# Where the gate projection runs in a two-block decoder kernel, and how eight PSUM banks are shared

## The chip, the cores and the metric

The kernel runs on one core of a Trainium2 chip. The metric is the device time of one launch in microseconds. Engines are named as the profile names them: PE is TensorE, DVE VectorE, ACT ScalarE, POOL GpSimd, SP the engine that issues the transfers. Each runs its own instruction stream in the order in which the program wrote it, and they meet at semaphores. PE writes only to PSUM, which has eight banks of 128 x 512 fp32.

## What is computed

Two decoder blocks on one sequence of 512 tokens, width 1024. The first block (its mixer is what the change touches):

```python
h = rms_norm(x, norm_mix)
q, kc, vc, ks, vs, kw, vw, gate_logits, hq, hf, hi, hg = split(h @ w_in)
o_nsa  = nsa_mixer(...)     # per query tile of 128: compressed, selected and window branch, softmax each
# HGRN mixer, 4 heads of 128:
q = silu(hq); f = lb + (1 - lb) * sigmoid(hf); k = 1 - f; v = hi
o_hgrn = rms_norm(gated_linear_recurrence(q, k, v, log f), o_gain) * silu(hg)
x = x + concat(o_nsa, o_hgrn) @ w_out
h = rms_norm(x, norm_ffn); gate, up = split(h @ w_gate_up)
x = x + (silu(gate) * up) @ w_down
```

Then a second block of two layers: stick-breaking and differential attention, and a squared-ReLU network. All large products are fp32-accurate: each operand is split into a rounded high part and a rest, and three products are summed.

## The kernel before

**Weights.** Every weight matrix is cut into units of 128 x 1024. A unit is loaded by SP into one of four `raw` buffers, cast by ACT into `whi`, and DVE writes the rest `raw - whi` into `wlo`; there are four pairs. Units come in the order in which the products use them.

**Products.** An input projection (list `IN1`, line 353) is a group of 512 columns: `hi`, `hf`, `hq`, `hg`, `cg` (compressed keys and values, and branch gates), `q`, `kv`. A group has four tiles (`cg` three), a tile four chunks of six matmuls. A tile accumulates in bank 0 or 1 in turn. "tok" groups have tokens on the partitions, "feat" groups features.

**Order.** The order of the instructions on every engine is computed in the program: `plan_first` (line 535) lists each step with its engine, a guessed duration, what it waits for, a priority and the rings from which it takes a buffer, and `Plan.run` schedules the steps greedily, the earliest possible start first, then the priority. The starts `T[...]` then only fix the order; each engine's program (`pe_program`, `act_program` and so on) merges its parts by them. So PE takes its steps in a fixed order, and waits if one is not ready.

**First mixer.** After the norm, the groups are projected. HGRN works head by head through `STEPS`: for each head a chain of small steps on DVE (`qm`, `hT`), POOL (`km`) and ACT (`qe`, `ke`), each with one set of PE products `hp`, then the sum over the values `pv1`, its squares `hsq`, the inverse root on POOL, and `hn` on DVE (line 2088), which writes the normed head into `mixR1`. The next head's PSUM reads come after `hn` on DVE. The gate hg is evacuated by ACT as a copy into `mixR1` and a sigmoid into `sqt`, and POOL multiplies the two, then multiplies by `hgain` (function `hg` of the POOL program, line 2438). `hn` waits for all four of those tiles and multiplies them in.

q and kv pass a preparation (norm per head, split, transposes). The sparse attention (NSA) starts when `hn` of head 3 and the kv tiles are there: logits on PE (`nlg`), maximum on DVE (`nmx`), exp on ACT (`nex`), scaling on POOL (`psc`), transposes on PE (`ptr`), split by ACT and DVE (`pth`, `ptl`), and the sums (`npv`) over value tiles. A query tile and key group (qi, g) owns one sum bank until `fc` (ACT) and `fin` (DVE) have read it; there are eight of them, (0, 0) to (3, 1).

The output projection has part 0 (HGRN half of the mixer, 8 chunks of 12 matmuls) and part 1 (NSA half, 8 chunks). It uses the place of the normed input, so its tiles (`mtr`, `mTh`, `mTl`, `mSh`, `mSl`) wait for the last input chunk, `LAST_IN`. Part 0 needs only HGRN. Then come the norm `f0` and the up projection of the first block.

**Banks in the first mixer.** 0 and 1: projection tiles. 4, 5: ring `T` for transposes. 2, 3, 6: ring `L` for HGRN products and attention logits. 7 and 1: ring `O` for sums; so output chunks before the tenth use bank 0 alone, and the tenth (n == 9) waits for `fin` (3, 1). The sums take bank 1 when the projections are over.

**Places.** `sqt` is one 128 x 512 scratch buffer shared in the order of the list `SQ`; hg is among its users.

Of the kernel before, what the change touches and what calls it, by code (L numbers as in the profile page):

```python
# [11 lines left out]
ALU = mybir.AluOpType  # L12
# [191 lines left out]
def decoder_program(nc, x_d, norm_mix, w_in, q_norm, k_norm, cmp_pos_k, cmp_pos_v, cmp_k_w1, cmp_k_w2,  # L204
# [86 lines left out]
    p1 = [r.t("p1_%d" % i, [128, 512]) for i in range(3)]  # L291
    r = Region(at_h, at_w)
    t1 = [(r.t("t1h%d" % i, [128, 512], F32R), r.t("t1l%d" % i, [128, 512], F32R)) for i in range(4)]
    p1 += [r.t("p1_%d" % i, [128, 512]) for i in range(3, 6)]
# [53 lines left out]
    def rows(w, nk):  # L348
        for k in range(nk):
# [29 lines left out]
    def dA(n):  # L379
        return 0.07 + 0.00084 * n  # L380
# [58 lines left out]
    SQ = [("hq", h) for h in range(4)] + [("hg", t) for t in range(4)] + [("q", t) for t in range(4)] + [("kv", t) for t in range(4)] + \  # L439
# [53 lines left out]
    def plan_op(P, m, fin, ring0):  # L493
        mk = "m%d" % m
        for n, (t, half, part) in enumerate([(t, half, 0) for half in range(2) for t in range(4)] + [(t, half, 1) for t in range(4) for half in range(2)]):
            unit = U["op", m, part, half]
            P.add(("op", (m, t, half, part)), "PE", 2.72, ("wlo", unit), ("wlo", unit + 1), *[("mSl" if part else "mTl", (mk, t, j)) for j in ((0, 1) if part else (2, 3))],
                  ("fin", (3, 1)) if m == 0 and n == 9 else None, seq="op", take=[(ring0 if n < 8 else "G", [("xadd", ("op", m, t, half, part))])])
# [13 lines left out]
    def plan_up(P, m):  # L512
        for part in range(2):
            for j in range(4):
                for i in range(4):
                    unit = U["up", m, 0] + j
                    P.add(("up", m, 0, part, i, j), "PE", 0.72, ("wlo", unit), *[("hTl", ("f%d" % m, t, 1)) for t in (2 * part, 2 * part + 1)], seq="gemm_up")
                    U_mm[unit] = ("up", m, 0, part, i, j)
# [14 lines left out]
    LAST_IN = {m: ("in", (m, "S1" if m else "kv", 3, 3)) for m in range(3)}  # L533

    def plan_first():
        P = Plan(T)
        P.ring("T", 2)
        P.ring("L", 3)
        P.ring("O", 2)
        P.rings["G"] = (2, [[("evV", (0, "hi", 0))], [("evV", (0, "hi", 1))]])  # L540
        P.ring("B0", 1)
# [10 lines left out]
        def sq_free(user):  # L552
            n = SQ.index(user)
            return (None if n == 0 else ("evV", (0,) + SQ[n - 1]) if SQ[n - 1][0] == "hq" else ("hgg", SQ[n - 1][1]) if SQ[n - 1][0] == "hg" else
                    ("fin", SQ[n - 1][1:]) if SQ[n - 1][0] == "fin" else ("psr", SQ[n - 1]))

        def evacs(name, i):
            k = (0, name, i)
            return [("evA", k)] if name in ("hf", "hg", "q") or (name, i) == ("cg", 2) else [("evV", k)] if name in ("hi", "hq") else [("evA", k), ("evV", k)]
        plan_in(P, 0, "n1", evacs)  # L560

        for i in range(4):
# [6 lines left out]
            P.add(("evA", (0, "hg", i)), "ACT", 2 * dA(512), last[3], sq_free(("hg", i)), pri=2)  # L569
            P.add(("hgg", i), "POOL", 2.6, ("evA", (0, "hg", i)))  # L570
# [47 lines left out]
        for h, lv in STEPS:  # L618
            k, before = (h, lv), (h, lv - 1)
            if lv < 0:  # L620
                P.add(("hk", h), "DVE", 0.46, ("fd", h), *([("hp", (h - 1, 5)), ("km", (h - 1, 6)), ("ke", (h - 1, 6))] if h else []), seq="hgrn", pri=4)
                P.add(("hp", k), "PE", 0.95, ("hk", h), ("evV", (0, "hq", h)), seq="hgrnT", pri=3, take=[("L", [("att", k)])])
                P.add(("att", k), "DVE", dV(512), ("hp", k), ("pv1", h - 1) if h else None, seq="hgrnV", pri=3)
            elif lv < 9:
# [11 lines left out]
                P.add(("hp", k), "PE", 0.95, ("qm", k), *([("km", k), ("qe", k), ("ke", k)] if lv else []), seq="hgrnT", pri=3, take=[("L", [("att" if lv < 7 else "aoc", k)])])  # L636
# [4 lines left out]
            else:  # L641
                P.add(("pv1", h), "PE", 2.6, ("att", (h, 6)), ("aoc", (h, 8)), *[("evV", (0, "hi", t)) for t in range(4)], seq="hgrnT", pri=3, take=[("L", [("hn", h)])])
# [7 lines left out]
        for it in NSA:  # L650
            i, qi, g, N, nh = it["i"], it["qi"], it["g"], it["N"], it["nh"]
            np_ = len(it["parts"])
            if it["kind"] == "cmp":
                if g == 0:
                    last = max([o["i"] for o in NSA if o["kind"] == "cmp" and o["qi"] == qi - 1], default=None)
                    P.add(("nlg", (i, 0)), "PE", 2.0, ("kch", 0), ("vcl", 0), ("pcpA", ("q", qi)), ("pcpV", ("q", qi)), *first, seq="nlg", pri=3, take=[("L", [("cad", qi)])])
# [5 lines left out]
            else:  # L662
                n = 0
                for r_, hs in enumerate(it["banks"]):
                    k = (i, r_)
                    P.add(("nlg", k), "PE", 0.09 + len(hs) * 2 * (N / 2400 + 0.014), ("pcpA", ("q", qi)), ("pcpV", ("q", qi)), ("pcpA", ("kv", qi)), ("pcpV", ("kv", qi)), *first,
                          seq="nlg", pri=3, take=[("L", [("nex", k)])])
# [17 lines left out]
        plan_op(P, 0, lambda kind, j, t: ("hn", 2 * j + 1) if kind == "D" else ("fin", (t, j)), "B0")  # L685
# [1935 lines left out]
```

## Time and profile before

| | us |
|---|---|
| median of 3 runs | 1974.48 (1973.38 to 1975.92) |
| the profiled execution | 1971.68 |
| its span | 1970.0 |
| PE matmul busy | 1933.9 (98%) |
| PE weight loads busy | 1622.3 (82%) |
| DVE busy | 968.8 (49%) |
| ACT busy | 790.6 (40%) |
| POOL busy | 257.5 (13%) |

The rows are of one execution. Busy time of PE is that of matmuls whose ends are modelled: a matmul of 512 columns shows 0.39 us and the next one starts 0.227 us after it, so small gaps do not show as idle, and start-to-start distances tell more. "[idle before <-releaser]" behind a row is time in which the engine stood still, and what ended it. Rows "x6" are merged. The granted clock is in shares of full speed, so 0.50 is 1.2 GHz and 1.00 is 2.4 GHz. Stages of the first mixer by the span's time: projections with HGRN from 12 to 222 us, attention 222 to 349, the rest of the output projection and the norm to about 380, the first block's network to 770; the second block's two layers follow.

### The profile page before, as it was taken

The page shows a single profiled execution, that of the slowest core. Times are in us where ns is not written, and L with a number is a line of the kernel's source. Part 1 is how long each engine was busy: PE and PEld are TensorE (multiplying, and loading weights), DVE is VectorE, ACT ScalarE, POOL GpSimd, SP SyncE. Part 2 cuts the span into 40 slices and gives each one's busy share as a digit, 9 for nine tenths or more (in the row PEclk, how much of TensorE's full clock was granted, in tenths as well). Part 3 has the DMA queues.
Part 4 walks back from the last instruction along what each step waited for, and adds up shares of the span by engine and source line. Part 5 has one row for each costly group of instructions (what it writes and reads, how often), then busy time and mean ns, then how long its engine had stood idle before and what let it go on. Part 6 is the DMA issues. An engine that isn't in the chain of part 4 may idle for free.

```text
span 1970.0 us, 24643 instructions
## 1 busy us (share of the span) xinstructions
PE 1933.9 (98%) x9842; PEld 1622.3 (82%) x9842; DVE 968.8 (49%) x1555; ACT 790.6 (40%) x1406; POOL 257.5 (13%) x334
## 2 busy tenths in 40 slices
PE   9999999999999999999999999999999899999998
PEld 7888787888888888877888888888878788888887
DVE  5546688432223357588642233337668852223334
ACT  4435566322223234377432332223547633333222
POOL 2133245000000010001011220001001102221000
PEclk9999999999999999999999999999999999999999
DMA  7211300133333322221133333332121123333331
GB/s 235 67 54 55 112 22 33 55 117 97 97 99 93 97 78 75 84 86 43 54 107 97 96 96 97 97 96 82 59 86 44 48 93 115 98 97 94 98 97 54
DMA packets 97138, 167.79 MB, mean 85 GB/s; under 512 B 8160, under 2 KB 49152, under 8 KB 97024
## 3 DMA queue, kind: packets, MB, share of 16 engines
q1 hardware_dynamic: 97024, 166.21, 27.5%
q8 instruction: 78, 1.28, 0.3%
q14 instruction: 36, 0.29, 0.0%
HBM read 164.09 MB, written 2.10 MB: 84 GB/s over the span
## 4 chain that ended last, share of the span: by engine, by line
PE 90%; DVE 5%; ACT 3%; issue 1%; DMA 0%; POOL 0%; SPq 0%; DVEq 0%; POOLq 0%; ACTq 0%
PE ps L49 86%; PE ps L52 4%; DVE wlo L71 1%; ACT sk1h L65 1%; DVE p L91 1%; DVE hTl L71 1%; ACT whi L65 0%; ACT p L62 0%; DVE x L71 0%; DVE t1l L71 0%; DVE small L82 0%; DMA raw<-in_w_in_dram 0%; DVE rot L71 0%; ACT hTh L65 0%; ACT t1h L65 0%
## 5 line engine op out<-in xcount | busy, mean ns | idle before, releaser
L65 ACT ACTIVATE whi<-raw 128x1024 fp32r<-128x1024 f32 x294 | 309.8, 1055 | 745.4 <-PE ps L49 742.5
L71 DVE TENSOR_TENSOR wlo<-raw,whi 128x1024 fp32r<-128x1024 f32 x294 | 361.3, 1230 | 417.2 <-ACT whi L65 414.5
L49 PE MATMUL ps<-hTh,whi 128*128 128x512 f32 (+1 forms) x1176 | 442.8, 377 | 0.0
L49 PE MATMUL ps<-hTh,wlo 128*128 128x512 f32 (+1 forms) x1176 | 438.0, 372 | 0.0
L49 PE MATMUL ps<-hTl,whi 128*128 128x512 f32 (+1 forms) x1176 | 437.9, 372 | 0.0
L49 PE MATMUL ps<-whi,uh 128*128 128x512 f32 x688 | 268.1, 390 | 0.0
L49 PE MATMUL ps<-whi,ul 128*128 128x512 f32 x688 | 267.8, 389 | 0.0
L49 PE MATMUL ps<-wlo,uh 128*128 128x512 f32 x688 | 267.8, 389 | 0.0
L49 PEld LDWEIGHTS ps<-hTh,wlo 128*128 128x128 f32 x1176 | 220.8, 188 | 39.6
L49 PEld LDWEIGHTS ps<-hTl,whi 128*128 128x128 f32 x1176 | 221.1, 188 | 36.9
L49 PEld LDWEIGHTS ps<-hTh,whi 128*128 128x128 f32 x1176 | 221.0, 188 | 36.6
L49 PE MATMUL ps<-whi,hTh 128*128 128x512 f32 x576 | 235.3, 409 | 3.0 <-DVE mixLT L71 1.6
L49 PE MATMUL ps<-whi,hTl 128*128 128x512 f32 x576 | 226.4, 393 | 0.0
L49 PE MATMUL ps<-wlo,hTh 128*128 128x512 f32 x576 | 225.8, 392 | 0.0
L71 DVE TENSOR_TENSOR ul<-u,uh 128x512 fp32r<-128x512 f32 x86 | 60.9, 711 | 281.2 <-ACT uh L65 281.2
L49 PEld LDWEIGHTS ps<-whi,uh 128*128 128x128 f32 x688 | 129.2, 188 | 26.8
L49 PEld LDWEIGHTS ps<-wlo,uh 128*128 128x128 f32 x688 | 129.2, 188 | 26.7
L49 PEld LDWEIGHTS ps<-whi,ul 128*128 128x128 f32 x688 | 129.2, 188 | 26.6
L49 PEld LDWEIGHTS ps<-whi,hTh 128*128 128x128 f32 x576 | 109.2, 190 | 24.3 <-DVE hTl L71 2.0
L49 PEld LDWEIGHTS ps<-whi,hTl 128*128 128x128 f32 x576 | 108.7, 189 | 23.9
L49 PEld LDWEIGHTS ps<-wlo,hTh 128*128 128x128 f32 x576 | 109.4, 190 | 19.2
L71 POOL TENSOR_TENSOR u<-gtmp 128x512 f32<-128x512 f32 x64 | 81.3, 1274 | 265.7 <-ACT gtmp L62 265.7
(232 smaller groups left out, 2156.7 us busy)
## 6 DMA issues: line engine op xcount, KB each, us to landing
raw<-in_w_ff_dram SPq DMA_DIRECT2D x128, 512.0 KB, 3.7
raw<-in_w_gate_up_dram SPq DMA_DIRECT2D x88, 256.0 KB, 3.1
raw<-in_w_in_dram SPq DMA_DIRECT2D x40, 512.0 KB, 4.5
raw<-in_w_in_dram SPq DMA_DIRECT2D x68, 256.0 KB, 3.1
raw<-in_w_down_dram SPq DMA_DIRECT2D x22, 512.0 KB, 3.6
raw<-in_w_o_dram SPq DMA_DIRECT2D x16, 512.0 KB, 3.7
x<-in_x_dram SPq DMA_DIRECT2D x8, 512.0 KB, 6.9
raw<-in_w_out_dram SPq DMA_DIRECT2D x8, 512.0 KB, 5.0
```

Of the source, the lines that this page charges most:

```text
L49: return self.eng.matmul(out, l, r, start=start, stop=stop, skip_group_check=True)
L52: return self.eng.transpose(out, in_, idn)
L65: return self.eng.activation(out, in_, ACT.Copy)
L71: return self.eng.tensor_tensor(out, a, b, op)
L91: return self.eng.tensor_tensor_scan(out, a, zero, 1.0, ALU.mult, ALU.add)
```

## The change

The group hg becomes the last of the input projections. Its sigmoid goes into one of two new buffers `sg`, DVE multiplies it by the tile in PSUM into the same buffer, and POOL multiplies `mixR1` by it once `hn` of head 3 is done. `hn` multiplies by `hgain` itself and no longer waits for the gate. The rings `T` and `L` become one ring of five banks in rotation; the sums have bank 7 alone; the output projection has banks 0 and 1 from its first chunk, and the wait for `fin` (3, 1) stands before the up projection and the transposes of norm `f0`. The load of the norm's gain is issued after `plo` (kv, 3) and not after the first chunk of part 1.

```diff
-    IN1 = [("hi", "tok", 4, [(2328, 512)]), ("hf", "feat", 4, [(1816, 512)]), ("hq", "feat", 4, [(1304, 512)]),
-           ("hg", "tok", 4, [(2840, 512)]), ("cg", "feat", 3, [(512, 256), (1280, 24)]), ("q", "tok", 4, [(0, 512)]),
-           ("kv", "tok", 4, [(768, 512)])]
+    IN1 = [("hi", "tok", 4, [(2328, 512)]),
+           ("hf", "feat", 4, [(1816, 512)]),
+           ("hq", "feat", 4, [(1304, 512)]),
+           ("cg", "feat", 3, [(512, 256), (1280, 24)]),
+           ("q", "tok", 4, [(0, 512)]),
+           ("kv", "tok", 4, [(768, 512)]),
+           ("hg", "tok", 4, [(2840, 512)])]
...
-    LAST_IN = {m: ("in", (m, "S1" if m else "kv", 3, 3)) for m in range(3)}
+    LAST_IN = {m: ("in", (m, "S1" if m else "hg", 3, 3)) for m in range(3)}
...
-        P.ring("T", 2)
-        P.ring("L", 3)
-        P.ring("O", 2)
+        P.ring("T", 5)
+        P.ring("O", 1)
         P.rings["G"] = (2, [[("evV", (0, "hi", 0))], [("evV", (0, "hi", 1))]])
-        P.ring("B0", 1)
...
-            P.add(("evA", (0, "hg", i)), "ACT", 2 * dA(512), last[3], sq_free(("hg", i)), pri=2)
-            P.add(("hgg", i), "POOL", 2.6, ("evA", (0, "hg", i)))
+            P.add(("evA", (0, "hg", i)), "ACT", dA(512), last[3], ("cm", (1, 3)), ("hgg", i - 2) if i >= 2 else None, pri=2)
+            P.add(("evV", (0, "hg", i)), "DVE", dV(512), ("evA", (0, "hg", i)), pri=2)
+            P.add(("hgg", i), "POOL", 1.0, ("evV", (0, "hg", i)), ("hn", 3), pri=4)
...
-                P.add(("hn", h), "DVE", 1.1, ("rs", ("hc", h)), *[("hgg", t) for t in range(4)], seq="hgrnV", pri=3)
+                P.add(("hn", h), "DVE", 1.1, ("rs", ("hc", h)), seq="hgrnV", pri=3)
...
-                yield T["op", (m, 0, 0, 1)] + 0.1
-                sp.wait_ge(*at("mm", ("op", m, 0, 0, 1)))
+                yield T["op", (m, 0, 0, 1)] + 0.1 if m else T["plo", ("kv", 3)] + 1.0
+                sp.wait_ge(*(at("mm", ("op", m, 0, 0, 1)) if m else at("plo", ("kv", 3))))
...
-        tring, lring, oring = Ring([4, 5]), Ring([2, 3, 6]), Ring([7, 1])
+        tring, lring, oring = Ring([4, 5, 2, 3, 6]), Ring([2, 3]), Ring([7])
+        fring = Ring([4, 5])
...
-                b = n % 2 if m or part else 0
+                b = n % 2
...
-                if m == 0 and n == 9:
-                    pe.wait_ge(*at("fin", (3, 1)))
...
+                            if j == 0 and g == 0 and m == 0:
+                                pe.wait_ge(*at("fin", (3, 1)))
...
-                        pe.wait_ge(*at("hn", 2 * j - 3))
+                        pe.wait_ge(*at("hgg", t))
...
-                    act.copyA(mixR1[:, i, :], ps[b][:, :]).then_inc(*up("hgc", i))
-                    sq_free(("hg", i))
-                    act.act(sqt[:, :], ps[b][:, :], ACT.Sigmoid).then_inc(*up("evA", key))
+                    if i >= 2:
+                        act.wait_ge(*at("hgg", i - 2))
+                    else:
+                        act.wait_ge(*at("cm", 1))
+                    act.act(sg[i % 2][:, :], ps[b][:, :], ACT.Sigmoid).then_inc(*up("evA", key))
...
+                elif name == "hg":
+                    dve.wait_ge(*at("evA", key))
+                    dve.tt(sg[i % 2][:, :], ps[b][:, :], sg[i % 2][:, :], ALU.mult).then_inc(*up("evV", key))
...
-                    for t in range(4):
-                        dve.wait_ge(*at("hgg", t))
+                    dve.wait_ge(*at("c", "all"))
                     c = cell(0, ("hc", h), 4)
                     for t in range(4):
-                        mr = mixR1[:, t, 128 * h:128 * h + 128]
-                        ins = dve.stt(mr, ps[bank("h", h, 9)][:, 128 * t:128 * t + 128], c[:, t:t + 1], mr, ALU.mult, ALU.mult)
+                        ins = dve.stt(mixR1[:, t, 128 * h:128 * h + 128], ps[bank("h", h, 9)][:, 128 * t:128 * t + 128], c[:, t:t + 1], hgain[:, :],
+                                      ALU.mult, ALU.mult)
...
-                pool.wait_ge(*at("evA", (0, "hg", t)))
-                pool.wait_ge(*at("hgc", t))
-                pool.tt(mixR1[:, t, :], mixR1[:, t, :], sqt[:, :], ALU.mult).then_inc(*up("hgm", t))
-                pool.wait_ge(*at("hgm", t))
-                pool.wait_ge(*at("c", "all"))
-                m3 = mixR1[:, t, :].rearrange("p (h d) -> p h d", h=4)
-                pool.tt(m3, m3, bc(hgain[:, :], 1, [128, 4, 128]), ALU.mult).then_inc(*up("hgg", t))
+                pool.wait_ge(*at("evV", (0, "hg", t)))
+                pool.wait_ge(*at("hn", 3))
+                pool.tt(mixR1[:, t, :], mixR1[:, t, :], sg[t % 2][:, :], ALU.mult).then_inc(*up("hgg", t))
```

## Rows read from the trace of the kernel before

**Rows 1.** The page: shares of the chain that ended last.

```profile
PE 90%; DVE 5%; ACT 3%; issue 1%; DMA 0%; POOL 0%; SPq 0%; DVEq 0%; POOLq 0%; ACTq 0%
```

**Rows 2.** Windows: stretch, length, busy of each engine, PE clock, DMA share, GB/s.

```profile
60.00:222.00 162.00, 161.72 (x948) 137.52 (x947) 93.24 (x198) 74.30 (x179) 50.41 (x63) 1.00 0.23 74
222.00:349.00 127.00, 117.83 (x742) 97.77 (x740) 97.06 (x220) 82.15 (x220) 51.46 (x57) 0.96 0.11 38
...
281.90:305.00 23.10, 23.10 (x134) 20.01 (x133) 16.73 (x30) 11.19 (x24) 7.28 (x8) 1.00 0.15 45
250.00:280.00 30.00, 28.33 (x193) 23.57 (x194) 27.91 (x72) 24.27 (x71) 15.70 (x18) 1.00 0.00 1
...
232.50:238.40 5.90, 5.90 (x22) 5.05 (x21) 1.89 (x9) 4.16 (x22) 3.13 (x3) 0.50 0.00 0
```

**Rows 3.** Timeline of PE, one cycle of query tile 3: start, length, instruction.

```profile
330.36 0.48 PE L49 MATMUL ps<-khh,qst 128*128 128x512 f32 x1
330.67 0.40 PE L49 MATMUL ps<-kll,qst 128*128 128x512 f32 x1
330.90 0.28 PE L49 MATMUL ps<-t1h,vst 128*128 128x256 f32 x1
...
331.38 0.60 PE L52 MATMUL ps<-ident,p 128*128 128x128 f32 x4
331.82 0.22 PE L49 MATMUL ps<-m_causal,identB 128*128 128x128 bf16 x1
```

**Rows 4.** Timeline of PE: HGRN; compressed keys' transposes; an output chunk, 302.30 to 305.02.

```profile
94.91 1.00 PE L49 MATMUL ps<-hQ,hK 128*128 128x64 f32 x8
...
121.97 1.11 PE L49 MATMUL ps<-hQ,hK 128*128 128x64 f32 x8
...
202.89 0.33 PE L52 MATMUL ps<-identR,kst 64*128 64x64 f32 x2
...
302.30 0.39 PE L49 MATMUL ps<-whi,hTh 128*128 128x512 f32 x1
...
305.02 0.28 PE L49 MATMUL ps<-t1h,vst 128*128 128x256 f32 x1
```

**Rows 5.** Groups by form, PE, 222.3 to 349.2: count | busy, mean ns | idle.

```profile
L52 PE MATMUL ps<-ident,p 128*128 128x128 f32 x160 | 25.8, 280 | 0.5 <-DVE hTl L71 0.5
L49 PE MATMUL ps<-t1h,vst 128*128 128x256 f32 x72 | 21.0, 312 | 2.3 <-DVE t1l L71 1.8
...
L49 PE MATMUL ps<-whi,hTh 128*128 128x512 f32 x36 | 15.3, 425 | 0.0
```

**Rows 6.** Timeline of PE: the longest wait; the last sums and what follows.

```profile
231.94 0.61 PE L49 MATMUL ps<-m_causal,identB 128*128 128x512 bf16 x1 [1.81 <-ACT p L62]
...
347.39 0.28 PE L49 MATMUL ps<-t1l,vst 128*128 128x256 f32 x1
349.23 0.50 PE L49 MATMUL ps<-whi,hTh 128*128 128x512 f32 x1 [1.56 <-DVE mixLT L71]
```

**Rows 7.** Timeline of DVE: `hn` of head 0.

```profile
120.79 1.13 DVE L79 SCALAR_TENSOR_TENSOR mixR<-ps,small,mixR 128x128 f32<-128x128 f32 x4 [1.29 <-POOL mixR L71]
```

**Rows 8.** Groups by form, 92 to 122: gate product, weight rest, hq.

```profile
L71 POOL TENSOR_TENSOR mixR<-mixR,sqt 128x512 f32<-128x512 f32 x4 | 5.2, 1293 | 11.7 <-ACT sqt L62 11.7
...
L71 DVE TENSOR_TENSOR wlo<-raw,whi 128x1024 fp32r<-128x1024 f32 x1 | 1.2, 1226 | 0.3 <-ACT whi L65 0.3
...
L71 DVE TENSOR_TENSOR hq<-ps,sqt 128x512 f32<-128x512 f32 x1 | 0.7, 692 | 1.9 <-ACT sqt L62 1.9
```

**Rows 9.** Timeline of POOL: an hgain product; a `wlo` ran from 118.12 to 119.50.

```profile
118.98 1.67 POOL L71 TENSOR_TENSOR mixR<-mixR,hgain 128x512 f32<-128x512 f32 x1
```

**Rows 10.** Timeline of ACT: the table load before the first exp.

```profile
39.07 1.28 ACT L62 ACT_TABLE_LOAD   x1
...
227.13 1.28 ACT L62 ACT_TABLE_LOAD   x1
228.43 0.42 ACT L62 ACTIVATE p<-p 128x256 f32<-128x256 f32 x1
```

More of the change, by code:

```diff
@@ L491, in plan_in, with plan_op @@
             U_mm[unit] = ("in", m, name, i, j)
-    def plan_op(P, m, fin, ring0):
+    def plan_op(P, m, fin):
         mk = "m%d" % m
@@ L497, in plan_op @@
             P.add(("op", (m, t, half, part)), "PE", 2.72, ("wlo", unit), ("wlo", unit + 1), *[("mSl" if part else "mTl", (mk, t, j)) for j in ((0, 1) if part else (2, 3))],
-                  ("fin", (3, 1)) if m == 0 and n == 9 else None, seq="op", take=[(ring0 if n < 8 else "G", [("xadd", ("op", m, t, half, part))])])
+                  seq="op", take=[("G", [("xadd", ("op", m, t, half, part))])])
             P.add(("xadd", ("op", m, t, half, part)), "DVE", dV(512), ("op", (m, t, half, part)), ("x", ("r", t)) if m == 0 and part == 0 else None,
@@ L516, in plan_up @@
                     unit = U["up", m, 0] + j
-                    P.add(("up", m, 0, part, i, j), "PE", 0.72, ("wlo", unit), *[("hTl", ("f%d" % m, t, 1)) for t in (2 * part, 2 * part + 1)], seq="gemm_up")
+                    P.add(("up", m, 0, part, i, j), "PE", 0.72, ("wlo", unit), *[("hTl", ("f%d" % m, t, 1)) for t in (2 * part, 2 * part + 1)],
+                          ("fin", (3, 1)) if m == 0 else None, seq="gemm_up")
                     U_mm[unit] = ("up", m, 0, part, i, j)
@@ L641, in plan_first @@
             else:
-                P.add(("pv1", h), "PE", 2.6, ("att", (h, 6)), ("aoc", (h, 8)), *[("evV", (0, "hi", t)) for t in range(4)], seq="hgrnT", pri=3, take=[("L", [("hn", h)])])
+                P.add(("pv1", h), "PE", 2.6, ("att", (h, 6)), ("aoc", (h, 8)), *[("evV", (0, "hi", t)) for t in range(4)], seq="hgrnT", pri=3, take=[("T", [("hn", h)])])
                 P.add(("hsq", h), "ACT", 1.3, ("pv1", h), seq="hgrnA", pri=3)
                 P.add(("rs", ("hc", h)), "POOL", 1.2, ("hsq", h), pri=1)
-                P.add(("hn", h), "DVE", 1.1, ("rs", ("hc", h)), *[("hgg", t) for t in range(4)], seq="hgrnV", pri=3)
+                P.add(("hn", h), "DVE", 1.1, ("rs", ("hc", h)), seq="hgrnV", pri=3)
         for t in range(4):
@@ L655, in plan_first @@
                     last = max([o["i"] for o in NSA if o["kind"] == "cmp" and o["qi"] == qi - 1], default=None)
-                    P.add(("nlg", (i, 0)), "PE", 2.0, ("kch", 0), ("vcl", 0), ("pcpA", ("q", qi)), ("pcpV", ("q", qi)), *first, seq="nlg", pri=3, take=[("L", [("cad", qi)])])
+                    P.add(("nlg", (i, 0)), "PE", 2.0, ("kch", 0), ("vcl", 0), ("pcpA", ("q", qi)), ("pcpV", ("q", qi)), *first, seq="nlg", pri=3, take=[("T", [("cad", qi)])])
                     P.add(("cad", qi), "DVE", 0.9, ("nlg", (i, 0)), ("ptr", (last, 0)) if qi else None, seq="nmx", pri=3)
@@ L854, in ev @@
         key = (m, name, i)
-        if name in ("hf", "hg", "q") or (name, i) == ("cg", 2) or (name in ("vD", "vS") and i % 2):
+        if name in ("hf", "q") or (name, i) == ("cg", 2) or (name in ("vD", "vS") and i % 2):
             return [("evA", key)]
@@ L1095, in norm @@
                     else:
-                        b, before = tring.take(("hTl", (key, t, half)))
+                        ring = fring if key == "f0" else tring
+                        if t == half == 0:
+                            fring.reset(("fin", (3, 1)), ("mTl", ("m0", 3, 3)))
+                        b, before = ring.take(("hTl", (key, t, half)))
                         for done in before:
@@ L1207, in hgrn @@
                 rel = ("hn", h) if lv == 9 else ("aoc", (h, lv)) if lv >= 7 else ("att", (h, lv))
-                b, before = lring.take(rel)
+                b, before = tring.take(rel)
                 for done in before:
@@ L1262, in nsa_logits @@
                     yield T["nlg", (it["i"], 0)]
-                    b, before = lring.take(("cad", qi))
+                    b, before = tring.take(("cad", qi))
                     for done in before:
@@ L1280, in nsa_logits @@
                     yield T["nlg", (i, r_)]
-                    b, before = lring.take(("nex", (i, r_)))
+                    b, before = tring.take(("nex", (i, r_)))
                     for done in before:
@@ L1910, in evac1 @@
             for name, kind, i, n, used in chunks(0):
-                if name in ("hf", "hg", "q") or (name, i) == ("cg", 2):
+                if name in ("hf", "q") or (name, i) == ("cg", 2):
                     continue
```

43 lines of the change are left out of this document (18 added, 25 removed).

## The prediction

> **What bounds the kernel now.** I read the page's busy table and chain first. TensorE's matmuls are busy for 98% of the span, as the table says, and it holds 90% of the chain that ended last [rows 1]. So time can come only from stretches in which TensorE does less than it could. The windows by stage show where they are: from 222 to 349 us, the sparse attention (NSA), matmuls are busy for 117.8 of 127 us and the granted clock is 0.96, while 281.9 to 305, where output-projection chunks lie between the attention steps, has no idle at all [rows 2]. After 372 us nothing that the change touches runs; its 1,600 us I take as equal.
>
> Busy time hides small gaps, because ends are modelled. So I counted the work of 222.3 to 349.2 by start-to-start distances. A full cycle of the last query tile [rows 3] gives 0.31 us for a khh matmul of 512 columns, 0.23 for the kll one, 0.12 for each 256-column sum, 0.44 for four transposes. A projection matmul takes 0.227: an output chunk of twelve runs from 302.30 to 305.02 [rows 4]. Times the counts, whose three largest forms are [rows 5]: 160 transposes 17.6 us, 144 sum matmuls 17.3, 109 projection matmuls (nine chunks of the output projection, 2.72 us each) 24.7, the 16 + 16 logit matmuls of 512 columns 8.6, 64 of the compressed keys at 0.11 7.1, 16 + 16 of 384 columns 7.0 (0.26 + 0.18), and the 18 smaller forms, some 200 instructions, 23.6. Sum 106 of 126.9 us: **21 us in which TensorE works below what its instructions need**. Named waits explain part (1.81 and 1.56 us, [rows 6]), half-rate clock another: the 5.9 us from 232.5 to 238.4 ran at a granted 0.50, that is 1.2 GHz, a loss of 3.0 [rows 2]. It came behind the wait that ended at 231.94.
>
> A second wait costs nothing today but sets the order. The four-head HGRN chain issues its matmuls at 94.91, then none until 121.97 [rows 4], because DVE's `hn` of head 0 (line 2088) waits for the POOL gate product of the last token tile [rows 7]: 16 gate chunks had to come first. TensorE is full meanwhile (161.7 of 162 us from 60 to 222, [rows 2]), so that stall is worth zero by itself.
>
> **The change part by part.** *Gate projection last.* 16 chunks of 6 matmuls, half an output chunk each, 16 x 1.36 = 21.8 us, leave the full stretch before the attention and enter the one with gaps. Since `hn` no longer needs the gate, head 1 goes on 27 us earlier (121.97 - 94.91, [rows 4]) and all heads are done well before kv, so q and kv end at 222.3 - 21.8 = 200.5 and the attention starts there. TensorE's total work is the same; what changes is how much of the 21 us is filled.
>
> *Is there enough filler?* Attention work without output chunks is 106 - 24.7 = 81 us. Filler is now gate 21.8, output part 0 21.8, and part 1 of token tiles 0 to 2 16.3: before, bank 1 belonged to the sums and the ninth output chunk was the last that could run before `fin` (3, 1); the change moves that wait to the up projection. Sum 141 us from 200.5, to 341.5, then 5.4 us of tile 3, against 349.2 plus seven chunks (19.0) before: 346.9 against 368.2, which is the 21 us again. The attention chain by itself took 127 us, less than 141, so TensorE sets the end, if its order written by the planner finds each step ready.
>
> *What cannot be filled.* The slice with filler had 0 idle, the dense 250 to 280 us 1.7 in 30 [rows 2]. I take the middle, 0.28 us per 10, over 141 us: 3.9, and the last handover to the mixer tiles, 1.8 [rows 6]. Together 5.7; bounds 1.8 and 9.8.
>
> *Other engines.* DVE takes four products from PSUM (0.69 each like hq's) and four wlo (1.23 each): 7.7 us more beside its 97.1 of 127 [rows 2, 8], now over 141: 74%, dense but with room. `hn` only changes an operand. ACT loses four copies and gains four weight casts in the stretch, and was busy for 82 of 127 us [rows 2]. POOL drops the four hgain products and does the other four (1.29 each, [rows 8]) after `hn`, hidden: its 51.5 us of the stretch leave it idle for over half. Behind a POOL wait for `hn` (3) or the gate stand the attention's scalings, but `hn` (3) is early then. SP: the reload of x waits for `pv1` (3) and comes earlier, the gain load moves to `plo` (kv, 3); the weights queued behind these waits have theirs met by then. Each zero; a late unit would cost its landing time.
>
> While POOL ran the hgain products, one that met a DVE wlo took 1.67 us, where the gate products take 1.29 [rows 8, 9]; that is 0.4 a meeting, at most 1.6 us in four, off the path. The Trainium skill, SBUF — State Buffer, section Who interferes with whom, says that a DVE tensor_tensor with both inputs in SBUF and a reading GpSimd instruction fully block each other; the four moved products would by that hold DVE for up to 5.2 us. The row shows a part of that.
>
> *The table loads, the cost that the diff does not show.* The gate's sigmoid now runs between the attention's exps. The trace has one ACT table load at 227.13, 1.28 us, just before the first exp, and none between 39 and 227 although sigmoid, square, tanh and copy alternate there [rows 10]. Each gate tile between exps costs two loads, four tiles 8 more: 8 x 1.28 = 10.3 us on ACT. TensorE's order is fixed and planned without them, so a late exp shows up as a wait there, like the 1.81 us at 231.94, the first logits behind that load. A step ready early waits up to one chunk of 1.36 us for TensorE, which hides some. Bounds: 0 and 10.3 exposed; I take half, 5.1. And one chance in two of a half-rate dip of 3.0 us: 1.5 (bounds 0 and 6, two dips).
>
> *Banks.* Five shared in rotation instead of 3 + 2: the same number, zero, bounds -1 and +2. One bank for sums: each of seven handovers needs ACT's copy and DVE's product, 347.39 to 349.23 in the trace [rows 6], 1.84 us; with filler to issue I take zero, the upper bound is a rival.
>
> Sum: 21 - 5.7 - 5.1 - 1.5 = 8.7 us. Span 1970.0 - 8.7 = 1961.3; the profiled execution took 1971.7 and the median of the runs is 1974.5, so I subtract from the median: 1965.8, and give **1966.0 us**.
>
> **The rivals.** (A) The loads hide under gate chunks and the clock stays up: 21 - 5.7 = 15.3, 1959.2; if even the filling is perfect, 1955.5. For it: ACT has 45 idle us in 127. Against: the 1.81 us wait behind the only load.
> (B) Every load is exposed and two dips follow, a wait on ACT's exps in the place of the gaps that the chunks fill: 21 - 5.7 - 10.3 - 6.0 = -1.0, 1975.5, reaching down to 1970. For it: fixed order, and the row at 231.94. Against: exps that wait behind TensorE anyway. The Trainium skill, ScalarE: Activation LUTs, section What ACT_TABLE_LOAD costs, gives 2.66 us for a switch with its drain. By it the eight cost 21.3 us, and all exposed the kernel would come out at about 1987. In this trace 1.30 us pass from the load's start to the exp's [rows 10], so the row speaks for half of that.
> (C) It does not do what it says: the attention starts no earlier, because PE's order takes gate chunks ahead of the compressed keys' transposes (202.89 us now, [rows 4]), and the gate simply precedes it: gain about 0, 1974.5.
> (D) Slower: the single sum bank. If each of seven handovers stalls TensorE for 1.84 us, 12.9 us go and 1966.0 becomes 1978.9; with a half-rate loss of 3.0 behind each, 34 us and 2000. It decides from 1.8 us each (8.7 + 3.9 = 12.6 us over seven). For it: from 250 to 280 DVE is 93% busy [rows 2], so its part of the handover can queue. Against: filler exists now at each.
>
> **How the numbers follow.** Forecast 0.50 (1960 to 1970), A 0.15, B 0.17, C 0.05, D 0.13. A measurement of this kernel tells 0.2%, 3.9 us, from no change. Faster than 1970.5: 0.50 + 0.15 + 0.02 of B = 0.67; within: 0.15 of B + 0.05 = 0.20; slower: 0.13. Range 1956 to 1976: it leaves out D and the tips of A and B, 0.17.
>
> **What would show it.** HGRN matmuls without a gap after 95 us and done before 170; first logits near 201 to 203; gate chunks between logits from 201 on; output chunks up to about 340; up to nine table loads from 200 to 245, and TensorE waits on ACT's exps near them. Part 1 of the output projection running before the last sums shows the freed bank. Wrong would be: logits starting after 210, TensorE waits for mixLT at each handover, a granted clock of 0.5 over more than 6 us, or any change after 372 us other than the shift.

## The result, and the profile after

The changed kernel takes 1961.24 us (median of four executions, 1960.28 to 1964.64); the kernel before, beside it, takes 1974.97 (1973.38 to 1975.92). The ratio is 0.9934 [0.9917, 0.9952], 13.0 us less. The prediction said 1966.0 with 1956 to 1976. Its profiled execution took 1961.46, of which the span is 1959.7, 10.3 less than the span before.

Busy times and chain of the page, kernel after (against [rows 1]):

```profile
PE 1930.2 (98%) x9842; PEld 1620.1 (83%) x9842; DVE 972.0 (50%) x1559; ACT 798.7 (41%) x1410; POOL 252.1 (13%) x330
...
PE 90%; DVE 4%; ACT 4%; issue 1%; DMA 0%; POOL 0%; SPq 0%; DVEq 0%; POOLq 0%; ACTq 0%
```

As before, these two lines say nothing of where the 10 us went. The windows by stage do (start:end and length, then busy time and count of PE, PEld, DVE, ACT and POOL, the granted clock, the DMA share and GB/s), kernel after:

```profile
60.00:200.00 140.00, 139.56 (x851) 119.28 (x850) 86.97 (x194) 65.87 (x166) 40.16 (x55) 1.00 0.23 71
200.00:280.00 80.00, 75.74 (x492) 62.78 (x491) 62.84 (x140) 63.94 (x160) 33.07 (x35) 1.00 0.17 53
280.00:345.00 65.00, 64.79 (x377) 55.17 (x376) 45.37 (x90) 35.50 (x81) 24.27 (x28) 0.97 0.14 41
```

The full stretch now ends near 200 instead of 222. What follows is the attention with its chunks: 4.5 us of idle in the 145 from 200 to 345, nearly all of it ahead of 280, where [rows 2] has 9.2 in 127; the clock is 1.00 and 0.97, against 0.96.

Timeline of PE, kernel after (start, length, instruction, idle before it and its releaser): the end of HGRN, the last transposes of kv, the first logits, the last two groups of sums, and the last transposes but one of norm `f0`:

```profile
164.14 0.83 PE L49 MATMUL ps<-hv,AO 128*128 128x128 f32 x6
...
201.55 0.50 PE L52 MATMUL ps<-identR,sth 128*128 128x128 f32 x4 [0.64 <-DVE stl L71]
...
203.69 0.48 PE L49 MATMUL ps<-kch,qst 128*128 128x32 f32 x3
...
341.20 0.28 PE L49 MATMUL ps<-t1l,vst 128*128 128x256 f32 x1
...
344.06 0.28 PE L49 MATMUL ps<-t1h,vst 128*128 128x256 f32 x1
...
344.54 0.40 PE L49 MATMUL ps<-whi,hTh 128*128 128x512 f32 x1
...
368.94 0.63 PE L52 MATMUL ps<-ident,htmp 128*128 128x128 f32 x4 [0.63 <-DVE htmp L79]
```

HGRN's last matmuls end at 165.0. The first logits of kch come at 203.69, where they came at 223.68 before: 20 us earlier. The sums end at 344.5 with eleven of sixteen output chunks issued (before: nine, at 347.5). The wait of 1.56 us behind the last sums in [rows 6] is gone: between 341.32 and 344.06 lies an output chunk, and at 344.54 the next one begins at once. The transposes of norm `f0` that stand at 368.94 stood at 379.23 before, 10.3 us later, and from there to the end both kernels take the same 1,590.8 us, as the prediction assumed.

### The profile page after: what moved, and what is told of

The parts are those of the page before. It is cut to its first block, busy times and chain, and to the rows that moved or that the text cites. A ratio compares the mean times of both kernels' runs of the same rounds, so it can differ in the third digit from the quotient of the medians.

```text
span 1959.7 us, 24657 instructions
## 1 busy us (share of the span) xinstructions
PE 1930.2 (98%) x9842; PEld 1620.1 (83%) x9842; DVE 972.0 (50%) x1559; ACT 798.7 (41%) x1410; POOL 252.1 (13%) x330
## 3 DMA queue, kind: packets, MB, share of 16 engines
q8 instruction: 78, 1.28, 0.3%
## 4 chain that ended last, share of the span: by engine, by line
PE 90%; DVE 4%; ACT 4%; issue 1%; DMA 0%; POOL 0%; SPq 0%; DVEq 0%; POOLq 0%; ACTq 0%
PE ps L49 86%; PE ps L52 4%; DVE wlo L71 1%; ACT p L62 1%; ACT sk1h L65 1%; ACT whi L65 1%; DVE p L91 1%; ACT L62 0%; DVE hTl L71 0%; DMA raw<-in_w_in_dram 0%; DVE x L71 0%; DVE rot L71 0%; ACT t1h L65 0%; ACT htmB L62 0%; ACT hTh L65 0%
## 5 line engine op out<-in xcount | busy, mean ns | idle before, releaser
L65 ACT ACTIVATE whi<-raw 128x1024 fp32r<-128x1024 f32 (+1 forms) x294 | 309.7, 1055 | 744.8 <-PE ps L49 741.2
L71 DVE TENSOR_TENSOR wlo<-raw,whi 128x1024 fp32r<-128x1024 f32 (+1 forms) x294 | 360.7, 1228 | 398.4 <-ACT whi L65 396.0
```

Source lines behind the costliest of these rows:

```text
L65: return self.eng.activation(out, in_, ACT.Copy)
L71: return self.eng.tensor_tensor(out, a, b, op)
```

## The experiments

Each ratio below is against the kernel before on the same chip, with its interval, and the us of a gain or a loss are worked out from the ratio; the two medians beside it can differ by another number. A difference of two ratios is uncertain by 3 to 4 us. I go first after the loads, then after the order and the banks. The changed kernel was timed once more, as the partner of the other runs.

> The changed kernel once more, as the base of this group of runs: 1961 us within 2 us, a gain of 13.7 us over the kernel before, if the first result holds.

Measured: 1963.3 us against 1973.63, ratio 0.9954 [0.9939, 0.9968], 9.1 us less; span 1959.5, the same picture. Together with the first timing the gain is between 9 and 13 us. The two intervals overlap; comparisons with the other experiments use this one.

### The table loads

**Without a table switch, sigmoid left out.** This kernel stores a copy in place of the sigmoid, so the gate isn't that of the reference; everything else stands.

```diff
-                    act.act(sg[i % 2][:, :], ps[b][:, :], ACT.Sigmoid).then_inc(*up("evA", key))
+                    act.copyA(sg[i % 2][:, :], ps[b][:, :]).then_inc(*up("evA", key))
```

> The changed kernel with a plain copy in the place of the gate's sigmoid, so the eight extra table loads are gone and nothing else in the order of the work changes. This leaves the sigmoid out of the computation. If the loads are hidden (rival A): 1961, no difference. If half of their 10.3 us is exposed, as the sum had it: 1956. If all is exposed (rival B) and the half-rate stretch behind the waits goes too: 1951 or less.

**The same product from tanh.** x · sigmoid(x) = x · (1 + tanh(x / 2)) / 2; the half goes into the HGRN norm's mean square and its eps.

```diff
-                    act.act(sg[i % 2][:, :], ps[b][:, :], ACT.Sigmoid).then_inc(*up("evA", key))
+                    act.act(sg[i % 2][:, :], ps[b][:, :], ACT.Tanh, scale=0.5).then_inc(*up("evA", key))
...
-                    dve.tt(sg[i % 2][:, :], ps[b][:, :], sg[i % 2][:, :], ALU.mult).then_inc(*up("evV", key))
+                    dve.stt(sg[i % 2][:, :], sg[i % 2][:, :], 1.0, ps[b][:, :], ALU.add, ALU.mult).then_inc(*up("evV", key))
...
-                rsqrt(cell(0, ("hc", h), 4), 1.0 / 128, ("hc", h))
+                rsqrt(cell(0, ("hc", h), 4), 4.0 / 128, ("hc", h), 4.0 * EPS)
```

> The changed kernel with the sigmoid as (1 + tanh(x/2)) / 2: ACT computes the tanh, DVE's one instruction adds 1 and multiplies by the tile in PSUM, and the factor 1/2 goes into the root of the HGRN norm on POOL. If tanh shares a table with exp, the eight loads go and the time is that of the copy version within 1 us. If it does not, the loads stay and the time is 1961.

**Eight more loads.** A sigmoid and an exp of one column ahead of each gate sigmoid.

```diff
+                    one = nsm[:, 52 + i:53 + i]
+                    act.act(one, ps[b][:, 0:1], ACT.Sigmoid).then_inc(*up("tiny"))
+                    act.wait_ge(sems.get("tiny", "tiny"), count["tiny"])
+                    act.act(one, one, ACT.Exp).then_inc(*up("tiny"))
+                    act.wait_ge(sems.get("tiny", "tiny"), count["tiny"])
                     act.act(sg[i % 2][:, :], ps[b][:, :], ACT.Sigmoid).then_inc(*up("evA", key))
```

> The changed kernel with one more pair of table loads for each gate tile (a one-column sigmoid and a one-column exp ahead of the gate's sigmoid): eight more loads, 10.3 us of ACT, and some 2 us of tiny instructions and waits. Loads hidden: within 2 us of 1961. Half exposed: 1967. Fully exposed: 1973 or more.

Measured: copy 0.9921 [0.9906, 0.9936], 1956.14 us; tanh 0.9922 [0.9906, 0.9937], 1956.4; eight more 1.0025 [1.0015, 1.0035], 1977.64. Timeline of ACT, kernel after, the loads around the first gate tile and the last:

```profile
213.60 1.28 ACT L62 ACT_TABLE_LOAD   x1
214.90 0.60 ACT L62 ACTIVATE sg<-ps 128x512 f32<-128x512 f32 x1
215.51 1.28 ACT L62 ACT_TABLE_LOAD   x1
216.81 0.37 ACT L62 ACTIVATE p<-ps,small 128x128 f32<-128x128 f32 x1
...
277.77 1.28 ACT L62 ACT_TABLE_LOAD   x1
279.07 0.58 ACT L62 ACTIVATE p<-ps,small 128x384 f32<-128x384 f32 x1
```

The groups by form of ACT from 200 to 345 us (count | busy, mean ns | idle) have this line in the kernel after:

```profile
L62 ACT ACT_TABLE_LOAD x9 | 11.5, 1283 | 0.2
```

and this one in the tanh kernel:

```profile
L62 ACT ACT_TABLE_LOAD x1 | 1.3, 1283 | 0.0
```

So the change adds exactly eight loads, two a gate tile, 10.3 us of ACT. PE's longest wait in the attention comes behind the last of them. Timeline of PE, kernel after, with the window that follows it:

```profile
277.92 0.39 PE L49 MATMUL ps<-t1h,vst 128*128 128x256 f32 x1 [0.72 <-DVE t1l L71]
...
279.79 0.66 PE L52 MATMUL ps<-ident,p 128*128 128x128 f32 x4 [1.37 <-ACT p L62]
...
281.76 0.69 PE L52 MATMUL ps<-ident,mixR 128*128 128x128 f32 x2 [0.19 <-ACT p L62]
```

```profile
280.00:290.00 10.00, 9.79 (x61) 8.67 (x60) 7.28 (x20) 6.21 (x20) 5.35 (x8) 0.83 0.18 52
```

The load at 277.77 holds the exp until 279.07, its transposes start at 279.79 after 1.37 us of wait, and the granted clock of the next ten microseconds is 0.83, which is a third of them at 1.2 GHz and 1.7 us lost. In the tanh kernel there is no such wait for an exp, but one of about the same length 2.6 us earlier, for `hTl` of DVE:

```profile
277.19 0.72 PE L52 MATMUL ps<-ident,mixR 128*128 128x128 f32 x4 [1.45 <-DVE hTl L71]
```

The last section says what held DVE there. The clock stays at 1.00 behind it, so a wait of this length need not bring the lower clock. The windows 200 to 280 and 280 to 345 of the tanh kernel read:

```profile
200.00:280.00 80.00, 77.53 (x522) 66.30 (x520) 66.07 (x149) 58.16 (x165) 37.25 (x40) 1.00 0.19 60
280.00:345.00 65.00, 65.00 (x373) 55.11 (x373) 44.95 (x86) 33.39 (x70) 22.19 (x27) 1.00 0.11 33
```

The eight loads are worth 0.9954 - 0.9922 = 0.0032, 6.3 us, and the means of the two kernels, timed side by side, differ by 6.4. Copy and tanh agree, so it is the loads and not the sigmoid's arithmetic. Eight further ones cost 1.0025 - 0.9954 = 0.0071, 14.0 us, more than their own 10.3. The edit adds more than loads: eight one-column instructions and the waits for them. In all ACT needs 4.29 us from the first load to the gate's sigmoid (213.47 to 217.76) where the kernel after needs 1.30, so 3.0 a tile or 12.0 in four. PE's waits of over 2 us from 200 to 345 in that kernel, and a window of it:

```profile
221.23 0.28 PE L49 MATMUL ps<-m_cmp,identB 128*128 128x256 bf16 x1 [2.91 <-ACT p L62]
...
244.78 0.58 PE L49 MATMUL ps<-t1h,vst 128*128 128x256 f32 x1 [2.81 <-DVE t1l L71]
...
276.70 0.39 PE L49 MATMUL ps<-t1h,vst 128*128 128x256 f32 x1 [3.29 <-DVE t1l L71]
...
295.01 0.39 PE L49 MATMUL ps<-t1h,vst 128*128 128x256 f32 x1 [3.79 <-DVE t1l L71]
```

```profile
240.00:260.00 20.00, 17.19 (x97) 15.51 (x96) 12.38 (x28) 14.03 (x32) 5.03 (x6) 0.74 0.00 1
```

One wait for each of the four gate tiles, 12.8 us together, and the clock falls to 0.74 behind the second; behind each of the other three follow 3 us or more at a mean of 0.54 to 0.58. From 200 to 380 us PE is idle for 3.1 us in the tanh kernel, 5.1 in the kernel after and 14.8 here. So the first eight loads partly hide in slack; the next eight find little left, and the clock's loss comes on top.

### The gate's place and the banks

**Banks alone.** The kernel before with the changed kernel's ring of five, its one sum bank and its two banks for all output chunks; the gate stays fourth.

```diff
-        P.ring("T", 2)
-        P.ring("L", 3)
-        P.ring("O", 2)
+        P.ring("T", 5)
+        P.ring("O", 1)
...
-        tring, lring, oring = Ring([4, 5]), Ring([2, 3, 6]), Ring([7, 1])
+        tring, lring, oring = Ring([4, 5, 2, 3, 6]), Ring([2, 3]), Ring([7])
+        fring = Ring([4, 5])
```

> The kernel before with the new banks alone: one ring of five, one bank for sums, output chunks on banks 0 and 1 with the wait for the last sums moved to the up projection. The gate projection stays fourth, and hn waits for it. By the filler account the five output chunks that may now run before the attention's end (13.6 us) fill the last query tile, and no table load is added: a gain of 8 to 11 us over before, 1963 to 1966. If the gate chunks are what fills the gaps (rival): 2 us or less. If the single sum bank stalls at its handovers (rival D): slower than before.

**Gate ahead of kv.** The changed kernel with its gate group one place earlier: HGRN is freed, yet all gate chunks precede the attention and no sigmoid falls between exps.

```diff
-           ("kv", "tok", 4, [(768, 512)]),
-           ("hg", "tok", 4, [(2840, 512)])]
+           ("hg", "tok", 4, [(2840, 512)]),
+           ("kv", "tok", 4, [(768, 512)])]
```

> The changed kernel with the gate projection before kv and not behind it: HGRN is freed from the gate and the banks are new, but no gate chunk lies in the attention, and its sigmoids come before the first exp, so there are no extra table loads. If HGRN's 27 us stall is worth nothing by itself, this is the time of the new banks alone within 1.5 us. If freeing HGRN helps by itself, it is faster than that by 3 us or more.

Measured: banks alone 0.9996 [0.9987, 1.0005], gate ahead of kv 0.9998 [0.9988, 1.0007]. To within 2 us neither does anything. In the second, HGRN's matmuls end at 164.9, as in the changed kernel: the removed stall of 27 us is worth zero, as predicted. The 8 to 11 us that I expected of the banks alone did not come. Both kernels have the same tail: 14 output chunks are issued before the sums end, and these end at 359.5. That is 12 us later than before, for five more output chunks of 2.72 us, 13.6 us in all: the chunks pushed the attention back nearly by their own length and did not fill its gaps. Timeline of PE, banks alone, the last sum and the waits of over 1.5 us after it:

```profile
359.44 0.28 PE L49 MATMUL ps<-t1l,vst 128*128 128x256 f32 x1
361.28 1.16 PE L52 MATMUL ps<-ident,htmp 128*128 128x128 f32 x8 [1.56 <-DVE mixLT L71]
...
372.71 0.66 PE L52 MATMUL ps<-ident,htmp 128*128 128x128 f32 x4 [1.93 <-DVE hTl L71]
```

The 32 us around the end of the attention as a window, first banks alone, then the kernel after:

```profile
344.00:376.00 32.00, 25.81 (x159) 21.23 (x158) 23.84 (x41) 20.36 (x39) 10.36 (x14) 0.95 0.17 53
```

```profile
329.00:361.00 32.00, 32.00 (x173) 27.23 (x172) 21.25 (x31) 15.15 (x25) 6.50 (x11) 1.00 0.13 35
```

With the shared ring, transposes of the mixer tiles get a bank early, so PE takes output chunks early, and by 344 only two of sixteen are left. The last tile's attention and the norm then run bare: 6.2 us of idle in 32, at a lower clock. In the kernel after, the gate chunks take the early places, five output chunks are left, and there is no idle.

**Separate rings again.** The changed kernel with transposes on banks 4 and 5 and logits on 2, 3 and 6; one sum bank.

```diff
-        tring, lring, oring = Ring([4, 5, 2, 3, 6]), Ring([2, 3]), Ring([7])
+        tring, lring, oring = Ring([4, 5]), Ring([2, 3, 6]), Ring([7])
```

> The changed kernel with the five banks split again, two for transposes and three for HGRN products and logits; one bank for sums. The sum gave the shared ring zero with bounds of -1 and +2, so 1962 to 1965. If sharing is what let the work interleave: slower than the changed kernel by 4 us or more.

**Two sum banks.** Ring of four, sums on 7 and 6:

```diff
-        tring, lring, oring = Ring([4, 5, 2, 3, 6]), Ring([2, 3]), Ring([7])
+        tring, lring, oring = Ring([4, 5, 2, 3]), Ring([2, 3]), Ring([7, 6])
```

> The changed kernel with two banks for sums (7 and 6) and a shared ring of four. If the handovers of the single sum bank cost nothing, as the sum had it, and a fifth bank in the ring matters little: 1963 within 2 us. If the handovers cost 1.8 us each (rival D): some 10 us faster than the changed kernel. If the ring needs its fifth bank: slower by 3 us or more.

**Ring of four, one sum bank.** Bank 6 is left unused:

```diff
-        tring, lring, oring = Ring([4, 5, 2, 3, 6]), Ring([2, 3]), Ring([7])
+        tring, lring, oring = Ring([4, 5, 2, 3]), Ring([2, 3]), Ring([7])
```

> The changed kernel with a ring of four banks (4, 5, 2, 3), bank 6 unused, one bank for sums. With the version that gives bank 6 to a second sum (1.0011 of before) it separates the two. If the single sum bank costs nothing: the same as that version within 2 us, and the fifth ring bank is worth some 10 us. If the second sum bank helps: slower than it by 3 us or more.

Measured: separate rings 0.9994 [0.9984, 1.0004]; two sum banks 1.0011 [1.0001, 1.0020]; ring of four 1.0010 [0.9999, 1.0020]. The last two differ only in the second sum bank, and agree within their intervals: the second sum bank is worth nothing here, and rival D is out. The fifth bank of the ring is worth 1.0010 - 0.9954 = 0.0056, 11 us, and sharing it 0.9994 - 0.9954 = 0.0040, 7.9 us. The small cost that the sum gave to the banks failed in both. The two losses look different. With the ring of four, the picture is that of banks alone: a wait of 4.03 us for ACT's p at 271.62, sums until 362.7, 14 output chunks before, then 1.57 and 2.17 us bare. With separate rings it is the other way round, as its timeline of PE and its windows before and after the last sums show:

```profile
333.83 0.38 PE L52 MATMUL ps<-ident,mixR 128*128 128x128 f32 x2
335.47 0.39 PE L49 MATMUL ps<-t1h,vst 128*128 128x256 f32 x1 [1.25 <-DVE t1l L71]
```

```profile
280.00:336.00 56.00, 51.82 (x304) 43.36 (x304) 37.52 (x84) 30.95 (x77) 23.71 (x26) 0.89 0.00 1
336.00:361.00 25.00, 25.00 (x115) 20.71 (x115) 12.29 (x17) 6.22 (x8) 1.49 (x3) 1.00 0.28 85
```

Output part 0 needs the transposes of the mixer tiles, sixteen of mixR. The tile view of PE for mixR, 200 to 345 us (count, duration, first and last start), with separate rings:

```profile
L52 PE MATMUL ps<-ident,mixR x16: 270/273/474, 281.8 to 333.9; 128*128 128x128 f32 x16
```

and in the kernel after:

```profile
L52 PE MATMUL ps<-ident,mixR x16: 272/310/473, 275.9 to 287.2; 128*128 128x128 f32 x16
```

They share banks 4 and 5 with the attention's transposes and take 52 us, from 281.8 to 333.9; in the ring of five they take 11, from 275.9 to 287.2. It is the same with the gate fourth: 52 us in the kernel before, with two banks (223.4 to 275.9), 11 with banks alone (224.5 to 236.0). Two banks did no harm as long as these transposes could start with the attention; now they wait for the last gate chunk. Only three output chunks are there for the attention, whose gaps stay open (4.2 us idle in 56, clock 0.89; this execution has a mean clock of 0.993 and took 1974.99 us, the slowest of eleven, so its clock is worse than the kernel's usual one), and thirteen run in one full block afterwards, when PE needs no filler.

**Separate rings without loads.** The tanh kernel with separate rings:

> The version without extra table loads (sigmoid through tanh) with the five banks split again into two and three. If the split rings lose because the mixer tiles' transposes cannot get a bank, the loss against the shared ring stays at some 10 us: 1966. If the split only lost because late exps held its banks, without the loads it loses under 3 us: 1957 to 1959.

Measured: 0.9957 [0.9944, 0.9971] (1965.12 us), 0.0035 or 6.9 us more than tanh on the shared ring. So the ring's worth does not hang on the loads, though 6.9 is less than the "some 10" expected.

**A planner that knows the loads.** The guessed duration of the gate's sigmoid raised by two loads:

```diff
-            P.add(("evA", (0, "hg", i)), "ACT", dA(512), last[3], ("cm", (1, 3)), ("hgg", i - 2) if i >= 2 else None, pri=2)
+            P.add(("evA", (0, "hg", i)), "ACT", dA(512) + 2.56, last[3], ("cm", (1, 3)), ("hgg", i - 2) if i >= 2 else None, pri=2)
```

> The changed kernel, with the sigmoid, and a planner that counts 2.56 us more for each of the four gate sigmoids, so that TensorE's order leaves room for the two table loads. If the loads cost because the fixed order does not know them, most of their 7 us comes back: 1957 to 1959. If ACT's time itself is what costs: 1962 to 1964, no change.

Measured: 0.9994 [0.9985, 1.0002], 0.0040 or 7.9 us worse than the changed kernel, where a gain was expected. The gate ends earlier (the first mixer transposes at 255.4 instead of 275.9), 14 output chunks go ahead of the last sums at 355.7, and the tail is bare again, with waits of 2.29, 1.03, 1.57 and 2.02 us from 348 to 369.

**Tanh with the gate chunks first.** The tanh kernel, and the plan's priority for gate chunks 4 instead of 5:

```diff
-                  seq="gemm", take=[("G", evacs(name, i))] if j == 0 and (m or used >= 4) else ())
+                  seq="gemm", pri=4 if (m, name) == (0, "hg") else 5, take=[("G", evacs(name, i))] if j == 0 and (m or used >= 4) else ())
```

> The tanh version with the gate chunks at priority 4 in the plan where other projection chunks have 5. Gate chunks then go ahead of steps of priority 5 that are ready at the same time, and the output chunks can start earlier. If the stall at 270 to 280 us, where the gate ends and the output tiles are not ready, is what is left: up to 2 us faster than 1956. If chunks too early only delay the attention: the same or slower.

Measured: 0.9914 [0.9900, 0.9927] (1956.15 us), not to be told from tanh alone. These two are the fastest versions that compute the whole, 15 to 17 us below the kernel before.

### All executions, split by the clock

Each execution comes with its time and PE's mean granted clock. (1 - clock) x time is what PE lost at most to the half rate; the rest is the time without it. Means over all executions of a kernel (the clock is known to 0.001, 2 us in one execution, which averages out). The end of the sums and the output chunks behind it are those of the profiled execution:

| kernel | n | sums end | output chunks after | time | lost to clock | rest |
|---|---|---|---|---|---|---|
| before (with the first four experiments) | 17 | 347.5 | 7 | 1972.5 | 11.8 | 1960.6 |
| before (with the middle four) | 33 | 347.5 | 7 | 1973.4 | 13.2 | 1960.3 |
| before (with the last four) | 21 | 347.5 | 7 | 1973.4 | 13.2 | 1960.2 |
| after, first timing | 4 | 344.5 | 5 | 1961.9 | 6.4 | 1955.5 |
| after, again | 6 | 344.3 | 5 | 1963.3 | 7.9 | 1955.4 |
| copy, sigmoid left out | 6 | 340.6 | 5 | 1956.9 | 5.2 | 1951.7 |
| tanh | 6 | 339.1 | 5 | 1956.9 | 5.5 | 1951.4 |
| tanh, gate chunks first | 4 | 340.8 | 5 | 1956.6 | 5.4 | 1951.2 |
| tanh, rings apart | 5 | 326.6 | 13 | 1964.9 | 5.9 | 1959.0 |
| eight more loads | 12 | 362.2 | 5 | 1977.7 | 14.5 | 1963.2 |
| banks alone | 11 | 359.5 | 2 | 1972.5 | 11.1 | 1961.3 |
| gate ahead of kv | 11 | 359.5 | 2 | 1972.8 | 10.8 | 1962.1 |
| rings apart | 11 | 336.1 | 13 | 1971.3 | 9.7 | 1961.6 |
| two sum banks | 11 | 355.9 | 2 | 1974.4 | 10.6 | 1963.8 |
| ring of four | 11 | 362.7 | 2 | 1975.5 | 10.8 | 1964.7 |
| planner knows loads | 11 | 355.7 | 2 | 1972.1 | 10.6 | 1961.5 |

The rest scatters little within a kernel (standard deviation 0.2 to 2.1 us). In the second timing a little over half of the changed kernel's gain is in it, 1960.6 - 1955.4 = 5.2 us. The other 11.8 - 7.9 = 3.9 us are clock: PE waits less and spends less time at 1.2 GHz. For the first timing no clocks of its partner are on record. The kernels with 2 or 13 chunks behind the sums all have a larger rest than the changed kernel with its 5, and those with the sigmoid also lose more to the clock; tanh with 13 has 7.6 us more rest than tanh with 5. But the number of chunks doesn't settle the rest: the kernel before has 7 and its rest is 5 us larger, and eight more loads cost 7.8 us of rest with 5.

## Why the prediction was right

**The start of the attention** moved as worked out: 20 us earlier for 21.8 predicted, first logits at 203.69 for "201 to 203". `hn` no longer waits for the gate, and that alone is worth zero.

**The filling** was the main term, 21 - 5.7 = 15.3 us. The tanh kernel shows it without the loads: 0.9922 is 15.4 us. That the two agree so closely is in part luck. By the table 9.2 us of it are rest and 6.3 clock, while the 21 held 3.0 of clock, so more was expected of the filling and less of the clock. And the agreement holds for the whole package only. The filler count of 141 us against an attention of 127 treated the gate and the output chunks as one sum, good wherever they lie. The runs show that it isn't so: banks alone added output chunks to the attention and gained 0; gate ahead of kv likewise; and with separate rings the same 141 us are on hand and 7 to 8 us of the gain are gone. The count also had 14 output chunks ahead of the last sums and 2 behind them. The changed kernel has 11 and 5, and every kernel here that does have 14 and 2 is no faster than the kernel before. What counts is when a chunk can be issued and, as far as the windows show, how many are left at the end.

**Banks** is therefore the step that failed: "five shared in rotation instead of 3 + 2: the same number, zero, bounds -1 and +2". Undoing the sharing costs 7.9 us, 6.9 without loads. I counted banks, and not who asks for them and when. The trace before had the mixer tiles' transposes spread over 52 us from the attention's first step on, and this could have been read: started behind the last gate chunk, at 276 to 282, the same 52 us end at 330, too late for part 0 to fill anything. The total came out because the 15.3 had silently assumed that output part 0 would be ready in time, which only the shared ring makes true.

**The single sum bank** at zero was right: the second one changes 1.0010 to 1.0011. PE's waits in the whole trace of after name no reader of the sums but `mixLT`, with 0.2 us against 1.6 before: none of the seven handovers stalls PE. That filler at each is the reason fits the timeline of the last one, and wasn't tested at the others.

**The table loads.** Count and length were right (eight, 1.28 us), the exposed share was taken as half, 5.1 us, with 1.5 for a dip of the clock behind them. Together 6.6; measured 6.3 by the ratios. By the table 4.0 of it are rest (1955.4 against 1951.4) and 2.4 clock, so both terms were near. That they lie between 213 and 278 instead of 200 and 245 is a miss: the gate chunks are spread over 70 us among the logits, and not issued in a row. The Trainium skill, ScalarE: Activation LUTs, section What ACT_TABLE_LOAD costs, has 1283 ns for the load, which the rows confirm, and 2.66 us for a switch with its drain, which they do not: from load to sigmoid pass 1.30 us (213.60 to 214.90) and from load to exp again 1.30 (215.51 to 216.81).

**The clock** was under-priced as a term. I weighed one dip of 3.0 us at one half and counted the 3.0 of the trace before within the 21. Over many executions the kernel before loses 12 to 13 us of its whole time to the lower clock. Its profiled execution, with a mean clock of 0.995, loses at most 9.9, of which two stretches in the attention are 5; a single trace shows one draw. This may be why the first timing gained 13.0 us and the spans of the two profiled executions differ by 10.3.

**POOL beside DVE.** The prediction read one hgain product of 1.67 us as a block in part, 0.4 a meeting, and left the other side out: the DVE subtraction beside it, of 560 columns, took 1.38 us (118.12), and one with no product beside it 0.74 (115.85). In the changed kernel one of the four moved products meets a subtraction, and it costs DVE 0.9 us (rows in the last section). That is less than the 5.2 of the upper bound, but whether it lies off the path, as predicted, was not tested.

The forecast of the sum was 8.7 us. The second timing gives 9.1 and the first 13.0; the forecast lies within the interval of the second (6.3 to 12.0 us) and just outside that of the first (9.5 to 16.4).

**Open.** The planner's greedy order turns small changes of a guessed duration or a ring into 2, 5 or 13 chunks behind the sums. That the number of chunks left is the cause, and not a companion, is argued from the windows; a kernel that fixes this number by hand with all else equal wasn't tried. Nor was the gate last tried with all banks as before: the version with separate rings keeps one sum bank and two banks for the output chunks. The kernel with two sum banks ran its profiled execution in 1968.7, 7 us below its own median, with a clock of 0.998 against 0.993 to 0.997 in the others. Its time without the clock's loss is that of the others, so the clock accounts for it; what kept the clock up isn't known.

## What to carry to other kernels

Moving an activation among others asks which table each needs; a function of the same table (tanh for sigmoid, with exp) made the move 6.4 us cheaper here. Work that fills gaps is worth something only if its inputs and banks are free in the gap, and the windows here speak for leaving some of it for the last gap: count it by time, not in total. Parts of a change can each measure zero and be worth 9 us together (banks alone 0.9996, the gate last on separate rings 0.9994, both 0.9954), so take each away from the whole as well as adding it to the kernel before.

## What the runs showed of the hardware

Before the first exp, sigmoid, tanh, square and copy alternate with no load between [rows 10], and so do exp and tanh: the tanh kernel has one load from 200 to 345 us, with four tanh of 128x512 among its exps. So tanh is in both tables. The Trainium skill, ScalarE: Activation LUTs, section Table sets: the hidden batching unit, lists it in the sets of exp and of sigmoid; the trace agrees.

The cost of a wait of PE is more than its length when the clock falls after it: eight loads of 10.3 us, with the small instructions beside them 12.0 us of ACT, cost 14.0, with 6.6 us more lost to the clock in the mean (14.5 against 7.9) and 7.8 us in the rest (1963.2 against 1955.4). These two are differences of means and come to 14.4.

A DVE subtraction that reads two SBUF tiles and a POOL product that does so too ran one behind the other, though their rows overlap. Timeline of DVE and POOL, kernel after, a weight rest without a product beside it and one that meets the last gate product:

```profile
273.34 1.22 DVE L71 TENSOR_TENSOR wlo<-raw,whi 128x1024 fp32r<-128x1024 f32 x1
...
277.61 1.27 POOL L71 TENSOR_TENSOR mixR<-mixR,sg 128x512 f32<-128x512 f32 x1 [0.76 <-DVE sg L71]
277.79 2.17 DVE L71 TENSOR_TENSOR wlo<-raw,whi 128x1024 fp32r<-128x1024 f32 x1
```

The product ends at 278.88 and the subtraction at 279.96, 1.08 us later: what it needed after the product was nearly its whole length. The tanh kernel has the same meeting (274.06, 2.18 us), and PE's wait of 1.45 us for `hTl` ends 1.0 us after that subtraction does. How much of this wait a product at another time would save wasn't tested.
